# A Fourier mixer on half the channels and half the tokens, in an fp32 transformer kernel on one core

## The reference

```python
def fourier_mix(u):                       # u: tokens x 1024, in 8 groups of 128 channels
    ug = u.astype(jnp.float32).reshape(B, S, F_GROUPS, F_GROUP_DIM)
    y = jnp.fft.fft2(ug, axes=(1, 3), norm='ortho').real
    return y.reshape(B, S, F_WIDTH)

def token_mix(h, w_in, w_fourier, w_ret, w_out):
    u_f, q, k, v, g, a_f, a_r = jnp.split(h @ w_in, offsets, axis=-1)
    y_f = fourier_mix(u_f) @ w_fourier
    y_r = retention_branch(q, k, v, g) @ w_ret
    merged = jax.nn.sigmoid(a_f) * y_f + jax.nn.sigmoid(a_r) * y_r
    return merged @ w_out
```

## Time and profile before

| | |
|---|---|
| time, median of 3 runs | 3159.14 us (3158.51 to 3160.34) |
| the profiled execution: its own time | 3160.31 us |
| the profiled execution: span | 3158.5 us |
| PE busy | 3052.7 us, 97% |
| DVE busy | 1785.3 us, 57% |
| ACT busy | 1130.7 us, 36% |
| POOL busy | 145.1 us, 5% |
| mean granted TensorE clock | 0.989 of 2.4 GHz |
| first layer, channel transforms with u and gates | 74 to 131 us |
| first layer, f | 131 to 153 us |
| first layer, yf with two gates | 153 to 207 us |

### The profile page before, as it was taken

The page is one execution under the profiler, slowest core; times in us unless marked ns, Lnnn a source line. Parts: engine busy times, 40 slices in busy tenths (PEclk is TensorE's granted clock), DMA queues, the critical chain, the costliest instruction groups (busy, mean ns, idle before and its releaser), DMA issues. The chain is left out here.

```text
span 3158.5 us, 36112 instructions
## 1 busy us (share of the span) xinstructions
PE 3052.7 (97%) x14822; PEld 2553.0 (81%) x14822; DVE 1785.3 (57%) x2538; ACT 1130.7 (36%) x1648; POOL 145.1 (5%) x130
## 2 busy tenths in 40 slices
PE   7999999999999999999999999999999998999998
PEld 5888888888778888878888889888898765778886
DVE  6566656766766567666755646323356655353234
ACT  3323332442334233332433434322234456332221
POOL 0001110000000000100000000000000014100000
PEclk9999999999999999999999999999999999999999
DMA  7354445343442343345322335222234230122221
GB/s 259 117 184 153 153 145 193 129 152 133 134 134 100 120 140 107 106 154 187 114 100 94 100 120 167 94 100 94 100 126 148 71 134 7 54 74 96 98 94 66
DMA packets 107204, 382.77 MB, mean 121 GB/s; under 512 B 11900, under 2 KB 13308, under 8 KB 107040
## 3 DMA queue, kind: packets, MB, share of 16 engines
q1 hardware_dynamic: 83280, 295.46, 27.9%
q10 hardware_dynamic: 23760, 85.01, 8.1%
HBM read 378.32 MB, written 2.10 MB: 120 GB/s over the span
## 5 line engine op out<-in xcount | busy, mean ns | idle before, releaser
L1657 DVE TENSOR_TENSOR WL<-stage,WH 128x1024 fp32r<-128x1024 f32 x535 | 657.4, 1231 | 671.7 <-ACT WH L1083 671.4
L400 PE MATMUL ps<-HH,WH 128*128 128x512 f32 x2188 | 857.9, 392 | 14.7 <-DVE HL L1699 5.2
L401 PE MATMUL ps<-HL,WH 128*128 128x512 f32 x2188 | 854.1, 390 | 0.0
L402 PE MATMUL ps<-HH,WL 128*128 128x512 f32 x2188 | 853.6, 390 | 0.0
L1083 ACT ACTIVATE WH<-stage 128x1024 fp32r<-128x1024 f32 x535 | 559.5, 1050 | 342.9 <-PE ps L402 331.5
L400 PE MATMUL ps<-GH,WH 128*128 128x512 f32 (+1 forms) x1652 | 586.6, 355 | 15.6 <-DVE WL L1657 9.4
L402 PE MATMUL ps<-GH,WL 128*128 128x512 f32 (+1 forms) x1652 | 584.3, 354 | 0.0
L401 PE MATMUL ps<-GL,WH 128*128 128x512 f32 (+1 forms) x1652 | 584.3, 354 | 0.0
L400 PEld LDWEIGHTS ps<-HH,WH 128*128 128x128 f32 x2188 | 412.3, 188 | 102.3 <-issue 9.0
L402 PEld LDWEIGHTS ps<-HH,WL 128*128 128x128 f32 x2188 | 412.1, 188 | 86.5
L401 PEld LDWEIGHTS ps<-HL,WH 128*128 128x128 f32 x2188 | 412.4, 188 | 83.0
(11 more groups left out here) (213 smaller groups left out, 2747.9 us busy)
## 6 DMA issues: line engine op xcount, KB each, us to landing
stage<-ws SPq DMA_DIRECT2D x535, 512.0 KB, 3.3
MST<-wm ACTq DMA_DIRECT2D x154, 512.0 KB, 3.3
Z<-wm SPq DMA_DIRECT2D x10, 512.0 KB, 6.8
TAB<-consts ACTq DMA_DIRECT2D x7, 448.0 KB, 3.5
MST<-wm SPq DMA_DIRECT2D x6, 512.0 KB, 6.3
out<-X SPq DMA_DIRECT2D x8, 256.0 KB, 2.1
X<-xT ACTq DMA_DIRECT2D x4, 256.0 KB, 5.4
X<-xT SPq DMA_DIRECT2D x4, 256.0 KB, 6.2
```

Source lines behind the costliest of these rows:

```text
L400: e.matmul(o, wh, mh, start=start, stop=False)
L401: e.matmul(o, wh, ml, start=False, stop=False)
L402: return e.matmul(o, wl, mh, start=False, stop=stop)
L1657: e.tensor_tensor(wl, src, wh.bitcast(F32), ALU.subtract).then_inc(wlo.sem, wlo.up(("w", i)))
```

## The change

Half of the channels and half of the tokens are computed, and w_fourier is folded to match.

- **Channel transform**: the tables are cut to 66 columns (64 channels, the middle one, one of padding). Four `mm3` of 66 columns, and one with a stationary tile of only two columns for token 256. The result is split by two instructions on ACT and two on DVE (64 channels into half a slot, the middle channel into slot 12), so that two groups share a stationary tile.
- **f**: four pairs of groups instead of eight groups, each one `mm3` of 512 columns, two of 258, one of 256; then `f64`, three `mm3` of 258 columns with 8 stationary columns for the middle channels. Tokens 0 to 256 stand in columns 0 to 256 of a bank, the odd part in 256 to 511.
- **Weights**: the token tables are cut to 7 and 4 blocks, still two chunks, and a third chunk `w_middle` (8 rows of it used) goes ahead of them into GH and GL slots 13 and 14, so the last table chunk is now the third ahead of f and not the second. Chunks grow by one in each layer, 535 to 537.
- **yf**: for each n two banks: `ya`, 4 `mm3` of 258 columns and one of 258 with 8 rows, and `yb`, 4 `mm3` of 256: 27 matmuls. ACT copies yb to SCR, DVE adds and subtracts with mirrored columns, copies tokens 0 and 256, and multiplies with Z.
- **Folding w_fourier**: rows c and 128-c arrive as two halves of a chunk. POOL adds them into an SCR buffer of the ring of three and subtracts them in place (two instructions of 128x512 for each of 16 chunks); ACT and DVE then split each half by itself.
- **Mods**: the `walk.tick()` beside each yf is gone, 8 in each layer. The same work is done by later ticks.

```diff
                     for t in range(4):
-                        cc = slice(0, 128) if t < 2 else slice(128, 256)
...
+                        cc = slice(0, 66) if t < 2 else slice(128, 194)
+                        mm3(p[:, t * 66:t * 66 + 66], uh[:, t * 128:t * 128 + 128], ul[:, t * 128:t * 128 + 128],
+                            CH[:, cc], CL[:, cc], t == 0, False, skip_group_check=True)
+
+                    inst = mm3(p[0:2, 132:198], uh[:, 512:514], ul[:, 512:514], CH[:, 0:66], CL[:, 0:66], False, True,
+                               skip_group_check=True)
...
-                for g in range(8):
-                    p = take_bank(("f", l, g), lo, "f", l, g)
-                    pe.wait_ge(lo, "cd", l, g)
-                    for t in range(4):
-                        inst = mm3(p[:, :], GH[:, 8 + g, t * 128:t * 128 + 128], GL[:, 8 + g, t * 128:t * 128 + 128],
-                                   *tabs[t], t == 0, t == 3)
-                    done(inst, ("f", l, g), *(held if g == 7 else []))
-                close()
+                block(*[("w_middle", l, 0, c * 128) for c in range(8)])
+                held = [("w", cur["n"])]
+                t01 = block(*[("dft", 0, 0, c * 128) for c in range(7)])
+                close()
+                t2 = block(*[("dft", 0, 128, c * 128) for c in range(4)])
+                tabs = [("w", cur["n"] - 1), ("w", cur["n"])]
+
+
+                for q in range(4):
+                    p = take_bank(("f", l, q), lo, "f", l, q)
+                    pe.wait_ge(lo, "cd", l, 2 * q + 1)
+                    st = [spectra(q, t) for t in range(4)]
+                    mm3(p[:, :], *st[2], *t2, True, False, skip_group_check=True)
+                    for t in range(2):
+                        mm3(p[:, 0:258], *st[t], *(x[:, t * 258:t * 258 + 258] for x in t01), False, False, skip_group_check=True)
+                    inst = mm3(p[:, 256:512], *st[3], *(x[:, 516:772] for x in t01), False, True, skip_group_check=True)
+                    done(inst, ("f", l, q), *held)
+                    held = []
...
-                    lin(("yf", l, n), 8, lambda k: ("w_fourier", l, k * 128, n * 128), slot, p[:, :],
-                        lambda k: ("f", l, k))
...
+                    for q in range(4):
+                        w = slice(512 + q * 128, 640 + q * 128)
+                        inst = mm3(pb[:, 0:256], wh[:, w], wl[:, w], GH[:, q, 256:512], GL[:, q, 256:512], q == 0, q == 3)
+                    ended(inst, ("yf", l, n))
...
-                    walk.tick()
-                    dve.wait_ge(mm, "yf", l, n)
+                    A, B = bank("ya", l, n), SA("yb", l, n)
+                    T = take(("ysum", l, n), dv, "yf", l, n)
+                    dve.wait_ge(ev, "yb", l, n)
+                    e.tensor_tensor(T[:, 1:256], A[:, 1:256], B[:, 1:256], ALU.add)
+                    e.tensor_tensor(T[:, 257:512], A[:, 255:0:-1], B[:, 255:0:-1], ALU.subtract)
+                    made(e.tensor_copy(T[:, 0:512:256], A[:, 0:512:256]), "ysum", l, n)
                     dve.wait_ge(ev, "gf", l, n)
-                    made(e.tensor_tensor(Z[:, n, :], bank("yf", l, n)[:, :], Z[:, n, :], ALU.mult), "yf", l, n)
+                    dve.wait_ge(dv, "ysum", l, n)
+                    made(e.tensor_tensor(Z[:, n, :], T, Z[:, n, :], ALU.mult), "yf", l, n)
...
+            def weight_sums(l, n):
+
+                i = upto["yf", l, n]
+                w = stage[:, i % NS, :]
+                before = sd.before("wsum", l, n)
+                if before:
+                    pool.wait_ge(signals[before[0]], *before[1])
+                pool.wait_ge(landed[i % NS], "w", i)
+                e.tensor_tensor(SD("wsum", l, n), w[:, 0:512], w[:, 512:1024], ALU.add)
+                e.tensor_tensor(w[:, 512:1024], w[:, 0:512], w[:, 512:1024], ALU.subtract).then_inc(pw.sem, pw.up(("wsum", l, n)))
```

More of the change, by code:

```diff
@@ L204, in program @@
         wlo, lo, dv, ssq, modv = (signal(n) for n in ("wlo", "lo", "dv", "ssq", "modv"))
[L205 removed]
+        plo, pssq, power, padd, pw = (signal(n) for n in ("plo", "pssq", "pow", "padd", "pw"))
         landed = [signal(f"ws{i}", 16) for i in range(NS)]
@@ L397, in close, with mm3 @@
                 cur["used"] = 8
[L399 to L402, removed]
+            def mm3(o, wh, wl, mh, ml, start, stop, **more):
+                e.matmul(o, wh, mh, start=start, stop=False, **more)
+                e.matmul(o, wh, ml, start=False, stop=False, **more)
+                return e.matmul(o, wl, mh, start=False, stop=stop, **more)
             def ended(inst, *names):
@@ L1145, in dft_high @@
                     act.wait_ge(mm, "cd", l, g)
-                    high(GH[:, 8 + g, :], bank("cd", l, g)[:, :], "cd", l, g)
+                    high(spectrum(GH, g), transform(bank("cd", l, g), 0, 64), "cd", l, g, 0)
+                    high(middle(GH, g), transform(bank("cd", l, g), 64, 65)[:, :, 0], "cd", l, g)
                 early = EARLY[l]
@@ L1195, in token_mix @@
                         fold_high(j + 2)
-                for g in range(8):
-                    weights(("f", l, g), ahead=1)
-                    act.wait_ge(mm, "f", l, g)
-                    high(GH[:, g, :], bank("f", l, g)[:, :], "f", l, g)
+                for q in range(4):
+                    weights(("f", l, q), ahead=1)
+                    act.wait_ge(mm, "f", l, q)
+                    high(GH[:, q, :], bank("f", l, q)[:, :], "f", l, q)
+                act.wait_ge(mm, "f64", l)
+                high(GH[0:8, 4, 0:258], bank("f64", l)[0:8, 0:258], "f64", l)
                 for n in range(8):
@@ L1203, in token_mix @@
                     weights(("yf", l, n))
-                    walk.tick()
+                    T = take(("yb", l, n), dv, "ysum", l, n)
+                    act.wait_ge(mm, "yf", l, n)
+                    e.activation(T[:, 1:256], bank("yb", l, n)[:, 1:256], ACT.Copy).then_inc(ev.sem, ev.up(("yb", l, n)))
                 def part_a(h):
@@ L1842, in token_mix @@
                         fold_low(j + 2)
-                for g in range(8):
-                    weights(("f", l, g), ahead=1)
-                    low(GL[:, g, :], bank("f", l, g)[:, :], GH[:, g, :], "f", l, g)
+                for q in range(4):
+                    weights(("f", l, q), ahead=1)
+                    low(GL[:, q, :], bank("f", l, q)[:, :], GH[:, q, :], "f", l, q)
+                low(GL[0:8, 4, 0:258], bank("f64", l)[0:8, 0:258], GH[0:8, 4, 0:258], "f64", l)
                 for n in range(8):
```

101 lines of the change are left out of this document (75 added, 26 removed).

## The result

| | before | after |
|---|---|---|
| time, median | 3159.74 us (4 runs, 3158.51 to 3160.74) | 3121.11 us (4 runs, 3118.27 to 3123.85) |
| the profiled execution: own time, span | 3160.31, 3158.5 us | 3123.03, 3121.0 us |
| PE busy | 3052.7 us | 3004.2 us |
| mean granted TensorE clock | 0.989 | 0.985 |

What follows compares the result with a forecast made beforehand. PE's matmul stream was taken to bound the kernel. Terms -65.0 + 7.0 + 3.4 + 5.3 - 6.0 + 1.0 = -54.3 us gave a forecast median of 3104.8 us, range 3096 to 3117.

Steps and rivals of the forecast that it cites:

- PE's stream: Fourier parts of both layers: fewer and narrower matmuls in f, yf and the channel transform save PE 65.0 us.
- transforms: Channel transform, both layers: only the three matmuls with two stationary columns get faster, -2.7 us, bounds 0 and -3.4.
- 15 x 0.121 + 12 x 0.120: PE time of one yf tile: 15 matmuls of 258 columns and 12 of 256, 3.25 us instead of 5.44.
- The column rule: PE matmuls: start-to-start time is 0.0133 plus columns / 2400 us, so 0.121 at 258 columns.
- Join: Ahead of f, both layers: PE waits for DVE's low part of the last table chunk, 3.5 us each, +7.0.
- clock, +3.4: Behind the wait ahead of f: PE at about half clock for 3.4 us in each layer, bounds 0 and 6.8.
- yf on the other engines: First layer's yf: POOL and DVE exclude each other, three tiles come 5.0 us apart, not 3.25; +5.3, bounds 0 and 11.
- First feed-forward: First layer, second half: fewer pairs with two-vector mods, so PE waits under 4 us; -6.0, bounds 0 and -8.2.
- Second feed-forward: Second layer: first two pairs get two-vector mods and the context's norm comes on top; +1.0, bounds 0 and +5.
- Some 5 us behind at most, again about what is absorbed: Second layer's feed-forward: DVE falls at most some 5 us behind, about what is absorbed; basis of the +1.0.
- the loop through POOL paces all of yf: Rival: sums exceed 1.3 us, so all 16 yf tiles take 4.8; 24.8 in place of 5.3, 3124.3 us, chance 0.08.
- The mods only move: Rival: first feed-forward keeps its wait, the second gets one of 5 us; 3114.8 us, chance 0.12.

Runs made afterwards that it cites:

- experiment 4: Changed kernel with the middle channels' yf matmuls on all 128 rows instead of 8, padded with zeros: 3115.31 us.
- experiment 3: Changed kernel with the w_middle chunk one gate earlier, so the last table chunk is again the second ahead of f: 3107.66 us, ratio to before 0.9832.
- Experiment 5: The kernel of experiment 4 with POOL's sums and differences of w_fourier left out, so part of the computation is missing: 3110.76 us.
- experiment 1: Kernel before with only the conditioning steps beside the 16 yf tiles taken out, later steps doing that work: 3167.22 us beside 3160.78, ratio 1.0022.

## Why the prediction was right in kind and wrong in size

Three things put the sum off: the second feed-forward (+1.0 in the sum, +8.9 measured), the matmuls with 8 rows in yf (6.2, priced as ordinary ones) and the second block (5.7, not in the sum). By its own steps:

- **PE's stream, -65.0**: came to -60.3. f and `f64` as worked out; transforms -4.2 in place of -2.7. The step that failed here is "15 x 0.121 + 12 x 0.120" for a yf tile: it took three matmuls with 8 rows for ordinary ones. 16 x 0.39 = 6.2 us too much. The column rule was right (experiment 4 has 3.25); that rows matter too was not in the sum, nor among the rivals. Of the two floors that the Trainium skill gives for small matmuls (TensorE: Matmul & The Clock Gate, "Back-to-back issue gap") the trace rules out the 62 ns, as the matmuls with two-column loads are 0.03 to 0.04 us apart; it fits the one of about 25 ns, without reaching it. The prediction took that floor for 66 columns, while the section has it for up to 64; by its formula for one matmul 66 columns take an estimated 30 ns. With 25 the estimate was -4.1, with 30 it would be -3.9; measured -4.2.
- **Join, +7.0, and clock, +3.4**: 6.4 and 3.4, by experiment 3. Read from the order of instructions and the earlier trace rows, and right.
- **yf on the other engines, +5.3**: 0.3. The exclusion is there, with DVE at 1.76 in place of 0.69, and what the Trainium skill says (SBUF — State Buffer, "Who interferes with whom") agrees. But DVE's tiles came 4.2 us apart on the mean (first sum at 147.87, fifth at 164.72), not 5.0, and PE's 3.64 apart, not 3.25, so that the lead of the converted chunks was enough (read from the distances, not tested). That is luck in part: it was the unforeseen price of the 8-row matmuls that slowed PE to what DVE could follow. Experiment 5 has the price at 3.25 us per tile: 2.9.
- **First feed-forward, -6.0**: -4.3, and -3.4 in experiment 1. Of the six waits of 0.5 to 0.9 two stayed (844.37 and 856.47), so 5.1 us of waits in all and not under 4, and the down tile's 3.4 didn't shrink: it is 3.36 to 3.38 in every kernel of this study, whatever the lag ahead of it.
- **Second feed-forward, +1.0**: +8.9. This is the largest miss. "Some 5 us behind at most, again about what is absorbed" fails twice. The two-vector mods at its start cost 2.2 us in four small waits at once, and the stretch of these pairs became 3.3 longer. And the norm's steps stand beside the last pairs, where a mod now stands too (12.30 us against 10.9), right ahead of a down tile that needs the last low part: nothing is left to absorb it, 3.66 us of wait and a stretch at half clock (1.7) follow.
- **The second block**, not in the sum: -5.7 against me. I had priced the clock at the wait that I added and left no room for a part with a short wait every 10 to 30 us, whose length varies between executions. Why it came out longer here stays open.

The profiled spans differ by 37.5 us, 16.8 less than the sum. Of these, 7.9 are from the second feed-forward, 6.2 from the rows, 5.7 from the second block, 1.7 from the first feed-forward and 1.5 from retention, less 5.0 from yf and 1.5 from the transforms: 16.5.

Of the rivals "the loop through POOL paces all of yf" (3124.3, chance 0.08) came nearest in time, by luck: yf had 0.3 us of waits in the first layer. "The mods only move" (3114.8, chance 0.12) was further off but has part of the right reason, a new wait in the second feed-forward; the first kept only part of its own.

## What to carry to other kernels

- Price a matmul by its rows as well as by its columns: where a few narrow ones stand between full ones, pad them with zeros to 128 rows before counting them as free.
- Background work that an edit displaces lands somewhere. Follow it to its new neighbours, and look at the pairs just ahead of the next place where one engine's last result is needed: there no lag is absorbed. Moving eight short steps to where DVE has room gave 5 us.
- A part with many short waits can take another time with the same instructions. Leave its spread, here some 5 us, in the range of any prediction, and don't read such a difference as an effect of an edit.

## What the hardware showed that I had not expected

- A change between matmuls with 128 rows and with 8 rows cost 0.19 us each way, spread over two gaps; one between 128 and 8 stationary columns cost nothing (0.12 and 0.13 apart).
- Exclusion holds up both sides: POOL's instructions of 1.26 to 1.29 us took 1.64 to 1.74 beside DVE's low parts, DVE's mod 2.30 instead of 1.28 beside POOL.
- Some 300 us of unchanged instructions took 307.9 to 313.4 us. In the five executions shown above PE's idle time there was 33.7 to 34.1 us, and the difference lay in its busy time.
- A wait of 1.93 or 1.94 us ahead of the same matmul was followed by full clock in one execution and by half clock in another.
